# Weighing the second one-hots of the gate stage on GpSimd and ScalarE, with VectorE left to compare

## The reference

```
sv, si = lax.top_k(s, PEER_TOPK)                 # 16 best of 128 keys, in each half
comb = sv[:, :, 0, :, None] + sv[:, :, 1, None, :]
fv, fi = lax.top_k(comb, PEER_TOPK)              # 16 experts for each of 8 heads
w = jax.nn.softmax(fv, axis=-1)
act = jax.nn.gelu(jnp.einsum("thkd,td->thk", u[eidx], tb))
return jnp.einsum("thk,thkd->td", (w * act).astype(tb.dtype), v[eidx])
```

## Time and profile before

| what | value |
|---|---|
| median of 3 runs | 5070.97 us (5063.25 to 5078.46) |
| the profiled execution, its own time | 5071.81 us |
| its span (first to last instruction) | 5070.0 us |
| VectorE busy over the span | 70% |
| ScalarE busy over the span | 36% |
| GpSimd busy over the span | 30% |
| TensorE busy over the span | 91% |

### The profile page before, as it was taken

The page is one execution under the profiler, slowest core; times in us unless marked ns, Lnnn a source line. Parts: engine busy times, 40 slices in busy tenths (PEclk is TensorE's granted clock), DMA queues, the critical chain, the costliest instruction groups (busy, mean ns, idle before and its releaser), DMA issues. The chain is left out here.

```text
span 5070.0 us, 83754 instructions
## 1 busy us (share of the span) xinstructions
PE 4601.9 (91%) x28889; PEld 4277.1 (84%) x28889; DVE 3568.5 (70%) x6872; ACT 1803.2 (36%) x3737; POOL 1496.6 (30%) x1358
## 2 busy tenths in 40 slices
PE   7999999688887989997988578999999999999997
PEld 5999999677776659896887567999999999999997
DVE  3101555454554652344899997999999999999996
ACT  3111333232322552223444693333333333333332
POOL 0000000111110000000000004777777777777773
PEclk9999999888888779997999799999999999999997
DMA  4332222223232324433999358999999999999996
GB/s 158 120 134 90 83 88 95 110 98 108 102 110 83 70 60 155 181 131 124 355 335 337 148 198 324 372 363 367 373 366 381 377 370 367 378 374 370 380 377 222
DMA packets 350790, 1170.27 MB, mean 231 GB/s; under 512 B 40128, under 2 KB 91456, under 8 KB 344256
## 3 DMA queue, kind: packets, MB, share of 16 engines
q0 software_dynamic: 147456, 536.94, 28.2%
q1 hardware_dynamic: 160480, 483.07, 26.5%
q10 hardware_dynamic: 42720, 148.52, 7.7%
HBM read 971.20 MB, written 197.46 MB: 231 GB/s over the span
## 5 line engine op out<-in xcount | busy, mean ns | idle before, releaser
L2198 POOL DMA_INDIRECT ex_vr<-in_expert_v,ex_at x512 | 610.9, 1193 | 225.9 <-issue 152.9
L2196 POOL DMA_INDIRECT ex_ur<-scr_u_rows,ex_at x512 | 573.6, 1120 | 296.6 <-issue 118.1
L2385 DVE SCALAR_TENSOR_TENSOR ex_acc_rows<-ex_vr,ex_wt,ex_acc_rows 128x1024 f32<-128x1024 f32 x512 | 648.7, 1277 | 1.0 <-DMA ex_vr<-in_expert_v,ex_at 0.6
L2377 DVE SCALAR_TENSOR_TENSOR ex_ur<-ex_ur,h_rows 128x1024 f32<-128x1024 f32 x512 | 615.3, 1216 | 21.5 <-DMA ex_ur<-scr_u_rows,ex_at 20.6
L2190 POOL COPY ex_at<-picked_at 128x4 uint32 x128 | 103.1, 805 | 1494.8 <-POOLq L125 1494.3
L933 POOL TENSOR_TENSOR sd_cts<-sd_cT,sd_ea 128x512 f32<-128x512 f32 x72 | 92.5, 1284 | 1427.6 <-ACT sd_ea L891 1427.6
L2208 PE MATMUL ex_ps<-hd_hi,ex_u_hi 128*128 128x320 f32 x2048 | 469.3, 310 | 18.2 <-PEq L125 16.4
L2208 PE MATMUL ex_ps<-hd_lo,ex_u_hi 128*128 128x320 f32 x2048 | 469.2, 310 | 0.0
L2208 PE MATMUL ex_ps<-hd_hi,ex_u_lo 128*128 128x320 f32 x2048 | 468.4, 310 | 0.0
L2299 ACT ACTIVATE ex_gel<-ex_dot 128x1 f32<-128x1 f32 x512 | 103.7, 203 | 903.5 <-DVE ex_ur L2377 903.5
L479 DVE TENSOR_TENSOR pr_w_lo<-pr_w,pr_w_hi 128x1024 fp32r<-128x1024 f32 x56 | 68.6, 1225 | 488.0 <-ACT pr_w_hi L475 488.0
(11 more groups left out here) (359 smaller groups left out, 11386.4 us busy)
## 6 DMA issues: line engine op xcount, KB each, us to landing
pk_raw_u<-in_expert_u SPq DMA_DIRECT2D x128, 512.0 KB, 6.5
scr_u_rows<-pk_rows_u ACTq DMA_DIRECT2D x128, 512.0 KB, 6.2
ex_u<-in_expert_u SPq DMA_DIRECT2D x128, 512.0 KB, 6.7
ex_v<-in_expert_v SPq DMA_DIRECT2D x128, 512.0 KB, 8.4
scr_gate<-gt_stage SPq DMA_DIRECT2D x10, 4096.0 KB, 12.6
ex_gate<-scr_gate SPq DMA_DIRECT2D x32, 1280.0 KB, 8.9
pr_w<-in_w_main SPq DMA_DIRECT2D x58, 512.0 KB, 4.6
scr_xbc<-pr_out ACTq DMA_DIRECT2D x32, 576.0 KB, 3.7
```

Source lines behind the costliest of these rows:

```text
L2196: nc.gpsimd.indirect_dma_start(out=ur[:, s], out_offset=None, in_=scr["u_rows"], in_offset=by).then_inc(ur_in[s], 16)
L2198: nc.gpsimd.indirect_dma_start(out=vr[:, s], out_offset=None, in_=io["expert_v"].rearrange("j i d -> (j i) d"), in_offset=by).then_inc(vr_ ...
L2377: v.scalar_tensor_tensor(out=ur[:, s], in0=ur[:, s], scalar=1.0, in1=rows[:, s], op0=ALU.mult, op1=ALU.mult, accum_out=dot[:, m:m + 1]).th ...
L2385: v.scalar_tensor_tensor(out=acc_g[:, s], in0=vr[:, s], scalar=wt[:, m:m + 1], in1=acc_g[:, s], op0=ALU.mult, op1=ALU.add).then_inc(row_r[ ...
```

## The change

All eight second one-hots are now compared in one VectorE instruction of 1024 columns, and VectorE's three instructions that compare and weigh are gone. ScalarE weighs four tokens instead of five. GpSimd weighs the other four in one product of 512 columns, in place, after waiting for `hot_r`. Since VectorE's last instruction of a batch no longer counts up `weighed_too`, a new semaphore `one1_r` tells TensorE that the first one-hots are there.

```diff
-    ON_ACT = 5
+    ON_ACT = 4
...
-                    v.tensor_tensor(one2[:, s, 0:ON_ACT], *keys(1, ON_ACT), ALU.is_equal).then_inc(hot_r[s], 1)
-                    v.tensor_tensor(one1[:, s], *keys(0, B), ALU.is_equal)
-                    for b in range(ON_ACT, B):
-                        last = v.tensor_scalar(one2[:, s, b], iota, cur[:, h, 1, at + b:at + b + 1], cur[:, h, 2, at + b:at + b + 1], ALU.is_equal, ALU.mult)
-                    last.then_inc(weighed_too[s], 1)
+                    v.tensor_tensor(one2[:, s], *keys(1, B), ALU.is_equal).then_inc(hot_r[s], 1)
+                    v.tensor_tensor(one1[:, s], *keys(0, B), ALU.is_equal).then_inc(one1_r[s], 1)
...
                     pe.wait_ge(weighed_too[s], i + 1 + START)
+                    pe.wait_ge(one1_r[s], i + 1 + START)
...
+        @block.gpsimd
+        def _(pool):
+            def turn(t):
+                for j in range(NBAT):
+                    s, u, h, at = batch(j)
+                    pool.wait_ge(hot_r[s], t * US + u + 1 + START)
+                    nc.gpsimd.tensor_tensor(one2[:, s, ON_ACT:B], one2[:, s, ON_ACT:B], cur[:, h, 2, at + ON_ACT:at + B].unsqueeze(2).to_broadcast([P, B - ON_ACT, P]), ALU.mult).then_inc(weighed_too[s], 1)
+
+            with pool.Fori(0, DT) as t:
+                turn(t)
```

More of the change, by code:

```diff
@@ L1984, in phase_gates @@
         cur_r, stored, ev = sem("gt_cur_r", 2), sem("gt_stored", 2), sem("gt_ev", 2)
-        hot_r, weighed, weighed_too, mm = (sem("gt_" + n, S) for n in ("hot", "weighed", "weighed_too", "mm"))
+        hot_r, one1_r, weighed, weighed_too, mm = (sem("gt_" + n, S) for n in ("hot", "one1", "weighed", "weighed_too", "mm"))
         u_in, u_hi = sem("gt_uin", E), sem("gt_uhi", E)
```

## The result

The changed kernel is slower: 5114.9 us median of 5 runs (5105.92 to 5129.19) against 5078.46 for 5 runs of the kernel before beside it, a ratio of 1.0079 (95% interval 1.0065 to 1.0092), which is 40 us of 5071 (the two medians differ by 36). A second set of runs on another occasion gave 1.0071 (1.0051 to 1.0091). The forecast was 59 us and 5130, with a range of 5108 to 5158. The direction and the mechanism held; the size was two thirds of the forecast.

A forecast was written before the change was run, and what follows sets the result against it. VectorE was taken to bound the stage; a batch going from 2.63 to 3.37 us (1.10 + 1.14 + 1.13), 80 times, adds 59 us, VectorE's 28 us gain included: 5130 us, range 5108 to 5158.

The forecast's parts named there:

- The bound: In the touched stage VectorE sets the pace, busy 119.80 of 120.00 us; no other stage overlaps it.
- VectorE alone: VectorE's two compares of 1024 columns take 2.28 us a batch unhindered, 28 us less over 80 batches.
- The collision: GpSimd's product and VectorE's compares with two SBUF inputs shut each other out: 1.09 us of standing still a batch.
- Rival 1: The compares, with repeated inputs, don't collide with GpSimd's product: stage 28 us shorter, 5043 us; chance 0.05.
- rival 2: Compares collide on one of two, or a third of the length: about 0.35 us a batch, a draw; chance 0.03.
- rival 4: GpSimd's product, its second input standing still along a row, is half as long again: 48 us more, 5178; chance 0.04.
- Who goes first: GpSimd's product gets its turn at the next seam between VectorE's compares, giving a round of 3.37 us a batch.
- Rival 3: Product and compares run fully serial, or GpSimd loses at seams: 3.55 us a batch, 5145 to 5153 us; chance 0.14.
- the product's own hold: GpSimd's product ends 1.13 us behind the compare it waited for, as L933's did; one term of the 3.37 us round.
- low end: In-place product with a repeated number a fifth shorter than L933 (0.25 us): 20 us come off, 5110.
- The signs that were named: What the profile after should show in the stage, such as VectorE's L2012 starting some 3.37 us apart.
- TensorE waiting for GpSimd: Sign in the stage's profile after: TensorE waits for GpSimd instead of ScalarE; no size given.

The follow-up runs named there:

- e1: Changed kernel with GpSimd's product cut to one column of each of its four tokens: batch 2.27 us, ratio 0.9948 to the kernel before.
- e3: Changed kernel with the compares' numbers 0 to 127 read from PSUM instead of SBUF: batch 2.26 us, ratio 0.9943 to the kernel before.
- e2: Changed kernel with the product's second input a row of numbers repeated for each token, not one weight along the row: batch 3.35 us, ratio 1.0110 to the kernel before.
- e6: The changed kernel run once more, unaltered, beside the kernel before: batch 3.11 us, stage 253.1 us, ratio 1.0071.
- e5: Kernel before, without GpSimd in the stage, its two wide compares reading the numbers 0 to 127 from PSUM: batch 2.63 us, ratio 1.0004.

## Why the prediction was right, and where it was too high

**The bound.** VectorE sets the stage's pace before and after, and no other stage moved. Right.

**VectorE alone.** The forecast was 2.28 us a batch if nothing hinders it; e1 and e3 measured 2.27 and 2.26. The 28 us of gain are real, and e1 and e3 show them in full (26 and 29 us).

**The collision.** That one long instruction shuts the other out was read off L1016 and L933 and holds here as it stood: a compare that is held ends 1.08 us behind the product's end (median; forecast 1.10), the next 1.14 after it. e3 settles that the two inputs in SBUF are the condition, which L1017 with its input in PSUM had pointed to the earlier trace rows. The Trainium skill's rule (SBUF — State Buffer, section "SBUF: two separate sides") names the same condition; by that rule, the runs agree, with 2.06 us for the compare in the changed kernel and 1.215 in e3. Rival 1 (compares with repeated inputs run free) and rival 2 (a third of the length) fall with the 2004 ns of L2012, and rival 4 (a longer product, since its second input stands still along the row) with the 0.90 us behind the compare and the 1.04 that the product takes unhindered in e3: it is shorter than L933, not longer.

The trace of the kernel before bears the collision out more broadly than the two cases of the earlier trace rows: 29 of the 56 L1016 start 0.08 us or more behind the start of a product of GpSimd's that still runs, and end 0.27 to 0.29 us behind its end, while 19 of the 56 L1017 run beside such a product and keep their 0.42. One of these stands right behind the L1016 of the earlier trace rows, while the product goes on until 1227.69:

```profile
1226.60 0.42 DVE L1017 TENSOR_TENSOR sd_h<-sd_h,sd_psY 128x256 f32<-128x256 f32 x1
```

**Who goes first.** That GpSimd gets in at the next seam was argued from two small copies. All 80 products do it in the changed kernel, at the seam behind L2013; e1 shows it most plainly. Rival 3, serial with lost turns and 3.55 us a batch, so falls too.

**The step that was mis-sized** is the product's own hold, "GpSimd's next product ends 1.13 behind that". It measured 0.90, 18 us over 80 batches. L933 was the nearest row, and e2 shows that it would have been exact for a second input that moves along the row, as L933's does. The prediction had this case as its low end ("a fifth shorter than L933", 5110), and the measured median, 5114.9, is near it. That the time lies inside the range owes something to luck: on that occasion the kernel before stood at 5078.46, 7.5 us over the 5070.97 from which the sum starts. In e6, beside 5072.59, the changed kernel had 5104.67, which is under the range's low end of 5108.

**A second, smaller term** was left out. The 2.63 us of the earlier trace rows is a batch without the `gt_cur` copy; that copy (0.34 us, each eighth batch) makes the kernel before some 4 us longer over the stage. In the changed kernel it falls into the time in which VectorE's next compare would stand still anyway:

```profile
2949.71 0.34 DVE L2009 COPY gt_cur<-ex_acc 128x192 f32 x1
...
2950.08 1.68 DVE L2012 TENSOR_TENSOR gt_one<-late_const,gt_cur 128x1024 f32<-128x1024 f32 x1
```

The compare behind the copy starts 0.37 us later than without one, and is 0.38 shorter (1.68 against 2.06): it ends when it would have ended. 80 x (3.12 - 2.63) is 39 us; less the 4, it is the 34 to 35 by which the stage grew.

**The signs that were named.** Starts 3.37 apart: 3.12. One compare at 1.22, the other at 2.2 to 2.3: 1.21 and 2.06. The product at 2.1 to 2.3: 1.95. All three miss the same way, for the one reason that the hold was 0.23 us shorter than L933's. ScalarE idle for over a third: it is 30% (83.57 of 120 us busy). The last copy near 3121 us: it ends at 3103.57, in an execution whose stage began 7.65 us later than before. TensorE waiting for GpSimd: that one was wrong, as the waits of the changed kernel show (engine, line, waited for, us in total, times, longest):

```profile
PE gt_ps L2032 <- ACT gt_stage L2060: 83.5, 78, 1.2
ACT gt_one L2052 <- DVE gt_one L2012: 79.7, 80, 3.5
```

What ends TensorE's wait is ScalarE's copy out of PSUM, and that copy stands in ScalarE's stream behind the weighing of the batch two ahead, which waits for the held compare. In the timeline of one batch above the copy ends at 2944.63 and the product at 2944.45, so the two are 0.2 us apart; in e2, where the product is longer, TensorE does wait for GpSimd:

```profile
PE gt_ps L2032 <- POOL gt_one L2041: 108.6, 79, 6.5
```

## What to carry to other kernels

Before work goes from VectorE to GpSimd to run beside it, look at the inputs of what stays: if VectorE's instructions read two tensors from SBUF, most of GpSimd's time is added to VectorE's (here 0.84 of 1.04 us), and the move pays only if it takes more than that off VectorE (here 0.37 us a batch, 2.64 to 2.27). That is shown for fp32 instructions with two tensor inputs on both engines; other forms weren't tried. One of VectorE's two inputs in PSUM took the collision away, and a small constant that every instruction reads is easily put there. An engine's busy share doesn't show this: compare the length of like instructions beside a working GpSimd and without, and price the collision with a row whose operands have the same pattern.

## What the runs showed of the hardware

- A GpSimd product whose second input stands still along the row ends 0.90 us behind the compare that it waited for with 512 columns and 1.33 with 768, 1.7 ns for each column added. The VectorE compare that it holds takes 2.06 and 2.48 us instead of 1.22, so it loses 0.84 and 1.27 us. With the second input moving along the row the product ends 1.13 us behind for 512 columns, a quarter more.
- Not all of a GpSimd product is hold: unhindered it lasts 1.04 us (e3), and it ends 0.90 us behind the compare that it waited for. From these two an estimate is that some 0.14 us at its start run beside VectorE; L933 gives the same (1.27 and 1.13 us).
- GpSimd's turn comes between two VectorE instructions that follow each other without a gap, and a hand-over costs next to nothing: a product of four columns ends 0.06 us behind the compare, and the batch takes 2.27 us (e1) where it takes 2.26 without a collision (e3).
- A VectorE compare of 1024 columns takes the same time with one input in PSUM (1.215 us in e3, 1.211 in e5) as with both in SBUF (1.216).
